# Layer normalisation around the mean of the first four feature blocks, its sums and squares added by TensorE between the last projections of the stage

## What is computed

```
def layer_norm(x, g, b):
    mu = jnp.mean(xf, -1, keepdims=True)
    var = jnp.mean(jnp.square(xf - mu), -1, keepdims=True)
    y = (xf - mu) * lax.rsqrt(var + LN_EPS)
    return y * g + b

x = layer_norm(ALPHA * x + m @ w_o, ln1_g, ln1_b)
h = jax.nn.silu(x @ w_gate) * (x @ w_up)
x = layer_norm(ALPHA * x + h @ w_down, ln2_g, ln2_b)
```

## Time and profile before

| | |
|---|---|
| median of 3 executions | 1194.69 us (1193.36 to 1196.69) |
| the profiled execution's own time | 1188.55 us |
| its span (first to last instruction) | 1186.7 us |
| PE busy in the span | 1039.2 us |
| mean granted TensorE clock | 0.936 of full speed |

### The profile page before, as it was taken

One profiled execution on the slowest core, in us unless ns is written; L12 is line 12 of the kernel. 1 busy time (PEld: TensorE's weight loads), 2 busy tenths in 40 slices (PEclk: granted clock), 3 DMA queues, 4 the chain that ended last, 5 costly groups with the idle time before them and its releaser, 6 DMA issues.

```text
span 1186.7 us, 22922 instructions
## 1 busy us (share of the span) xinstructions
PE 1039.2 (88%) x7438; PEld 965.6 (81%) x7438; DVE 555.3 (47%) x1070; ACT 495.1 (42%) x902; POOL 770.9 (65%) x1077
## 2 busy tenths in 40 slices
PE   5997798977798999999889968899669799999994
PEld 5996577765787999999779947787558699999993
DVE  2997946435624232210249987543446332222003
ACT  4333345533436544433353232654334364444334
POOL 6998216622493989998559971455127569999882
PEclk9988789988898999999989987999779989999997
DMA  8646458421152664444256534674002324444441
GB/s 305 219 164 216 128 179 281 169 92 54 43 191 82 212 238 163 177 160 169 81 183 219 172 96 133 207 266 174 36 36 102 129 108 160 172 167 160 175 145 76
DMA packets 78140, 185.07 MB, mean 156 GB/s; under 512 B 9283, under 2 KB 42435, under 8 KB 77507
## 3 DMA queue, kind: packets, MB, share of 16 engines
q1 hardware_dynamic: 74130, 171.22, 41.4%
q10 hardware_dynamic: 3744, 11.40, 2.7%
q0 software_dynamic: 144, 0.96, 0.2%
HBM read 170.97 MB, written 12.57 MB: 155 GB/s over the span
## 4 chain that ended last, share of the span: by engine, by line
POOL 63%; issue 35%; POOLq 1%; DMA 1%; ACT 0%; SPq 0%
POOL w_lo L567 57%; POOL hid L590 3%; POOL res L588 2%; POOLq L561 0%; DMA table<-page_table_in 0%; DMA wch<-weights_in 0%; POOLq L585 0%; POOLq L147 0%; POOL hid L588 0%; ACT w_hi L974 0%; POOL hid L591 0%; SPq L429 0%; POOLq L573 0%; SPq L170 0%; POOLq L578 0%
## 5 line engine op out<-in xcount | busy, mean ns | idle before, releaser
L567 POOL TENSOR_TENSOR w_lo<-wch,w_hi 128x256 fp32r<-128x256 f32 x940 | 705.8, 784 | 404.6 <-ACT w_hi L974 402.9
L627 PE MATMUL proj<-x_hi,w_hi 128*128 128x288 f32 x1376 | 416.7, 303 | 39.3 <-DVE x_lo L1598 17.3
L628 PE MATMUL proj<-x_hi,w_lo 128*128 128x288 f32 x1376 | 411.4, 299 | 0.0
L629 PE MATMUL proj<-x_lo,w_hi 128*128 128x288 f32 x1376 | 410.9, 299 | 0.0
L974 ACT ACTIVATE w_hi<-wch 128x1024 fp32r<-128x1024 f32 x235 | 248.3, 1057 | 230.3 <-PE proj L629 118.3
L627 PEld LDWEIGHTS proj<-x_hi,w_hi 128*128 128x128 f32 x1376 | 263.7, 192 | 51.1 <-issue 27.2
L628 PEld LDWEIGHTS proj<-x_hi,w_lo 128*128 128x128 f32 x1376 | 264.5, 192 | 0.0
L629 PEld LDWEIGHTS proj<-x_lo,w_hi 128*128 128x128 f32 x1376 | 263.9, 192 | 0.0
L1295 DVE SCALAR_TENSOR_TENSOR hid<-u_p,sm,hid 128x256 f32<-128x256 f32 x240 | 164.6, 755 | 3.4 <-DVE sq L1324 1.0
L645 PE MATMUL proj<-hid_lo,w_hi 128*128 128x288 f32 x352 | 104.2, 296 | 0.0
L643 PE MATMUL proj<-hid_hi,w_hi 128*128 128x288 f32 x352 | 103.8, 295 | 0.0
(11 more groups left out here) (236 smaller groups left out, 1298.3 us busy)
## 6 DMA issues: line engine op xcount, KB each, us to landing
wch<-weights_in SPq DMA_DIRECT2D x235, 512.0 KB, 3.2
pg<-cmp_pages_in SPq DMA_DIRECT2D x128, 128.0 KB, 2.6
pg<-slc_pages_in SPq DMA_DIRECT2D x128, 128.0 KB, 2.1
wn<-win_in SPq DMA_DIRECT2D x4, 2048.0 KB, 8.4
win_out<-wn ACTq DMA_DIRECT2D x4, 2048.0 KB, 8.1
hid<-w_in SPq DMA_DIRECT2D x2, 1024.0 KB, 5.9
kv_out<-kv ACTq DMA_DIRECT2D x2, 864.0 KB, 5.4
res<-xT_in SPq DMA_DIRECT2D x1, 1152.0 KB, 5.1
```

What stands on the lines that cost most here:

```text
L567: last = nc.gpsimd.tensor_tensor(lo[:, cols], raw[:, cols], hi[:, cols].bitcast(F32), ALU.subtract)
L627: mm(ps, hi[:, kb], x_hi[:, kb], start=kb == 0, stop=False)
L628: mm(ps, lo[:, kb], x_hi[:, kb], start=False, stop=False)
L629: last = mm(ps, hi[:, kb], x_lo[:, kb], start=False, stop=kb == KD - 1)
```

## The change

TensorE's sums move from behind the last projection to between the projections. To make that possible before the mean is known, the blocks are first shifted by an estimate of the mean, that of the first four blocks ("seed"): variance = mean of squares of the shifted values, minus the square of their mean. PE adds one seed matmul behind each of the projections 1 to 4, four square matmuls behind projection 5, and a mean and a square matmul for two blocks each behind projections 6 and 7 (`features_behind`): 4 + 4 + 8 = 16 for a normalisation. DVE subtracts the seed mean from the blocks as they come (`shifted`), forms the variance in one step (`var_ready`), and later subtracts the mean of the shifted values two blocks at a time, interleaved with the scaling and with `low`, which is `low_features`. ACT squares blocks 0 to 3 in two steps and 4 to 7 one by one, between the `high_part` calls. Three `warm` activations on one element per partition place the loads of the root's and of tanh's tables. In the down stage `high_part` of the next layer's chunks 0 and 1 come ahead of the last square. The convolution's normalisation does the same work under new names. The lines below leave blank lines and the signals' declarations out.

```diff
@@ -258,7 +259,9 @@
         ps_g = ps_t[:, 1, :]
         turn_ps = [ps_s[:, 0, :], ps_s[:, 1, :], ps_g] * 2
-        stat_ps = [a[:, 0:TOK] for a in (ps_g, ps_m, ps_s[:, 0], ps_s[:, 1], ps_s[:, 0], ps_s[:, 1])]
+        conv_mean, conv_var = ps_g[:, 0:TOK], ps_m[:, 0:TOK]
+        seed_ps, mean_ps, square_ps = ps_g[:, 0:TOK], ps_s[:, 0, 0:TOK], ps_s[:, 1, 0:TOK]
+        SEED = KD // 2
         def k(name):
             return cst[:, CONST[name]]
@@ -672,14 +678,46 @@
...
+            def seed_part(layer, which, kb):
+                o = (O_WO, O_DOWN)[which] + kb
+                pe.wait_ge(*out_read[o % 2](layer, o // 2 + 1))
+                last = mm(seed_ps, k("mean_c"), resv[:, kb], start=kb == 0, stop=kb == SEED - 1)
+                if kb == SEED - 1:
+                    stat_done.up(last)
+            def mean_part(layer, which, kb):
+                pe.wait_ge(*shifted(layer, 6 * which + kb - 1))
+                last = mm(mean_ps, k("mean_d"), resv[:, kb], start=kb == SEED, stop=kb == KD - 1)
+                if kb == KD - 1:
+                    stat_done.up(last)
+            def square_part(layer, which, kb):
+                pe.wait_ge(*squared(layer, 2 + 6 * which + (kb // 2 + 1 if kb < SEED else kb - 1)))
+                last = mm(square_ps, k("mean_d"), sqv[:, kb], start=kb == 0, stop=kb == KD - 1)
+                if kb == KD - 1:
+                    stat_done.up(last)
+            def features_behind(layer, which, n):
+                if 0 < n <= SEED:
+                    seed_part(layer, which, n - 1)
+                if n == SEED + 1:
+                    for kb in range(SEED):
+                        square_part(layer, which, kb)
+                if n > SEED + 1:
+                    for kb in (2 * n - 8, 2 * n - 7):
+                        mean_part(layer, which, kb)
+                        square_part(layer, which, kb)
@@ -932,22 +970,14 @@
-                for which in range(2):
-                    if which == 0:
-                        for n in range(KD):
-                            project_x(layer, O_WO + n, CH_IN + CH_MIX + n, 0 if n == 0 else None)
-                        first = O_WO
-                    else:
-                        for n in range(2 * KF):
-                            project_x(layer, O_GU + n, CH_IN + CH_MIX + CH_WO + n, KD if n == 0 else None)
-                        for n in range(KD):
-                            down(layer, n)
-                        first = O_DOWN
-                    def summed(kb):
-                        pe.wait_ge(*out_read[(first + kb) % 2](layer, (first + kb) // 2 + 1))
-                    statistics(layer, KD, resv, k("mean_d"), summed)
-                    statistics(layer, KD, sqv, k("mean_d"), lambda kb: pe.wait_ge(*squared(layer, 3 + 4 * which + kb // 2)))
+                for n in range(KD):
+                    project_x(layer, O_WO + n, CH_IN + CH_MIX + n, 0 if n == 0 else None)
+                    features_behind(layer, 0, n)
+                for n in range(2 * KF):
+                    project_x(layer, O_GU + n, FIRST_GU + n, KD if n == 0 else None)
+                for n in range(KD):
+                    down(layer, n)
+                    features_behind(layer, 1, n)
@@ -1031,17 +1061,30 @@
...
-                    act.wait_ge(*centered(layer, (4 * which - 2 if which else 0) + part + 1))
-                    do(sq[:, cols], source[:, cols], ACT.Square, squared, wait=False)
-            def norm_sd_root(layer, which):
...
+            def features_square(layer, which, n):
+                blocks = slice(2 * n, 2 * n + 2) if n < 2 else slice(n + 2, n + 3)
+                act.wait_ge(*shifted(layer, 6 * which + n + 1))
+                do(sqv[:, blocks], resv[:, blocks], ACT.Square, squared, wait=False)
+            def features_root(layer, which):
+                act.wait_ge(*stat_done(layer, 3 * which + 4))
+                do(sqv[:, 0], mean_ps, ACT.Square, mean_squared, wait=False)
+                act.wait_ge(*var_ready(layer, which + 1))
+                do(rstd, rstd, ACT.Sqrt, sd_ready)
@@ -1221,8 +1264,14 @@
                             do(x_hi[:, c], gate_a[:, c], ACT.Copy, x_hi_ready, wait=False)
                             if c % 2:
                                 high_part(layer, CH_IN + (KD + c) // 2 + PAIRS)
-                        for n in range(CH_IN + CH_MIX + PAIRS, CH_IN + CH_MIX + CH_WO + PAIRS):
-                            high_part(layer, n)
+                        for n in range(KD):
+                            high_part(layer, CH_IN + CH_MIX + PAIRS + n)
+                            if n == SEED:
+                                do(warm[:], eps[:, 0:1], ACT.Sqrt, wait=False)
+                                features_square(layer, 0, 0)
+                                features_square(layer, 0, 1)
+                            if n >= SEED:
+                                features_square(layer, 0, n - 2)
                     else:
                         for i in range(KF):
                             act.wait_ge(*out_done(layer, O_GU + 2 * i + 1))
@@ -1236,13 +1285,20 @@
                             if i == 2:
                                 act.wait_ge(*x_lo_ready(layer, 2 * KD))
                                 do(res[:], res[:], ACT.Copy, ax_ready, scale=ALPHA)
-                        for n in range(CHUNKS - CH_DOWN + PAIRS, CHUNKS):
-                            high_part(layer, n)
-                        high_part(layer + 1, 0)
-                    norm_sd_squares(layer, 1 + which, res[:], KD)
-                    if which == 1:
-                        high_part(layer + 1, 1)
-                    norm_sd_root(layer, 1 + which)
+                        do(warm[:], eps[:, 0:1], ACT.Sqrt, wait=False)
+                        n = SEED
+                        for c in range(CH_DOWN - 1):
+                            if n < KD - 1 and 8 * c + 7 >= KF * (n + 1) + 8:
+                                if n == SEED:
+                                    features_square(layer, 1, 0)
+                                    features_square(layer, 1, 1)
+                                features_square(layer, 1, n - 2)
+                                n += 1
+                            j = CHUNKS - CH_DOWN + PAIRS + c
+                            high_part(*((layer, j) if j < CHUNKS else (layer + 1, j - CHUNKS)))
+                        assert n == KD - 1
+                        features_square(layer, 1, n - 2)
+                    features_root(layer, which)
                     gn, bn = (s("g1"), s("b1")) if which == 0 else (s("g2"), s("b2"))
                     for c in range(KD):
                         if c % 2 == 0:
@@ -1253,6 +1309,7 @@
                             do(x_hi[:, c - 1], resv[:, c - 1], ACT.Copy, x_hi_ready, wait=False)
                     act.wait_ge(*x_ready(layer, KD * which + KD))
                     do(x_hi[:, KD - 1], resv[:, KD - 1], ACT.Copy, x_hi_ready, wait=True)
+                    do(warm[:], eps[:, 0:1], ACT.Tanh, wait=False)
                 high_part(layer + 1, 2)
                 act.sem_inc(act_order.sem, ACT_ORDER - act_order.count)
                 act_order.count = ACT_ORDER
@@ -1345,20 +1402,61 @@
...
-            def center(layer, which, source, n):
-                dve.wait_ge(*stat_done(layer, 2 * which + 1))
-                ps = stat_ps[2 * which]
-                for part in range(n // 2):
-                    two = source[:, 2 * part:2 * part + 2]
-                    do(v.tensor_tensor(two, two, ps.unsqueeze(1).broadcast_to([P, 2, TOK]), ALU.subtract), centered, wait=False)
-                dve.wait_ge(*centered(layer, centered.count))
-            def normalise(layer, which, source, n):
-                dve.wait_ge(*sd_ready(layer, which + 1))
...
+            def scale(two):
+                do(v.tensor_tensor(two, two, rstd.unsqueeze(1).broadcast_to([P, 2, TOK]), ALU.mult), normed, wait=False)
...
+            def features_norm(layer, which, low):
+                first = (O_WO, O_DOWN)[which]
+                dve.wait_ge(*ax_ready(layer, which + 1))
+                for n in range(KD):
+                    o = first + n
+                    dve.wait_ge(*out_done(layer, o + 1))
+                    read_out(o, v.scalar_tensor_tensor(out=resv[:, n], in0=bank[o % 2][:, 0:TOK], scalar=0.5, in1=resv[:, n],
+                                                       op0=ALU.mult, op1=ALU.add), wait=n >= SEED)
+                    if n == SEED:
+                        dve.wait_ge(*stat_done(layer, 3 * which + 3))
+                        for c in range(0, SEED, 2):
+                            two = resv[:, c:c + 2]
+                            do(v.tensor_tensor(two, two, seed_ps.unsqueeze(1).broadcast_to([P, 2, TOK]), ALU.subtract), shifted, wait=False)
+                    if n >= SEED:
+                        do(v.tensor_tensor(resv[:, n], resv[:, n], seed_ps, ALU.subtract), shifted, wait=n == KD - 1)
+                def subtract(c):
```

(38 more changed lines are left out.)

51 lines of the change are left out of this document (29 added, 22 removed).

## The result

| | before | after |
|---|---|---|
| median of the executions | 1191.88 us (1188.19 to 1196.69, 8) | 1202.78 us (1195.64 to 1208.44, 8) |
| the profiled execution's own time | 1188.55 us | 1201.59 us |
| its span | 1186.7 us | 1199.7 us |
| mean granted TensorE clock | 0.936 | 0.929 |

The ratio of the times is 1.0086, 95% interval [1.0058, 1.0114]: the change makes the kernel slower by 10.2 us (0.0086 x 1191.88). The forecast was +4.5 us.

A forecast was written before the change was run, and what follows sets the result against it. PE was taken to bound the projections, a chain of dependent steps the tails. Behind w_o +0.85 twice, boundary +0.65 and end +2.15 gave +4.5 us on the median 1194.69, so 1199.2 us; range 1193.0 to 1203.5.

The forecast's parts named there:

- 12 sums between projections, a stage: PE's full projection stream: 12 of 16 sum matmuls now stand between projections at 0.49 us each, 5.9 us added.
- six switches of format, a stage: PE going from fp32 sums back to fp32r projections: 0.05 us each, six times a stage, 0.3 us added.
- tail, T to scaling: From PE free behind the last projection (T) to first scaling: 5.65 us instead of 12.31, 6.65 us saved.
- restart behind w_o: First matmuls after the pause behind w_o: gaps and a later return of the clock cost 1.3 us a stage.
- boundary stage, T to the end of the last `x_lo`: Layer boundary: 6.65 us saved to scaling, 1.1 given back by the later last `x_lo`, the clock not counting.
- tail of the last stage, T to the span's end: Kernel end: 6.65 us saved, 1.1 given back, 1.5 added by a tanh table load ahead of the last `high_part`.
- The failed step: ACT's root table load (1.28 us) and squares of blocks 0 to 6, placed between `high_part` calls, cost nothing.
- the low bounds: Whole kernel, lower bounds everywhere (0.485 us a matmul, no switch cost, 0.5 for the restart): +1.3 us.
- the high ones: Whole kernel, upper bounds (0.25 us a switch, 2.5 for the restart): +11.7 us.
- That moved sums hide: Rival: slack in PE's stream hides the moved matmuls; free of charge, some 20 us gained, 1174. Chance 0.14.
- A clock low for longer: Rival: each of three restarts costs another 3 us or so at half speed; about +10 us, 1205. Chance 0.12.
- A tail that doesn't shorten: Rival: in the down stage a late load delays `high_part` and the last square; 3 us twice, +10, 1205. Chance 0.06.

The follow-up runs named there:

- e2: The changed kernel with the tile `warm` declared last, so all other tiles lie where they do in the kernel before; ratio 1.0050, +6.0 us.
- e11: The kernel before plus 12 unused fp32 matmuls of constants a stage where the change puts its sums, its own sums left in place; ratio 1.0172, +20.5 us.
- e1: The kernel before plus the unused one-element tile `warm` ahead of the constants, moving every later tile by 32 bytes; ratio 1.0034, +4.0 us.
- e12: The kernel before plus the unused tile declared right ahead of `w_hi`, so the weight tiles move and the constants and chunks stay; ratio 1.0046.
- e6: The kernel before plus ten matmuls of constants in the pause behind the squares' sums of each stage; ratio 1.0013.
- e8: The kernel before with feature normalisation squares rounded to fp32r and summed by fp32r matmuls, all sums still behind the last projection; ratio 0.9995.
- e5: e2 plus twelve fp32 matmuls of constants, results unused, in the pause behind the sums of each stage; ratio 1.0049.
- e3: e2 without the activation that loads the table of tanh early; ratio 1.0025.
- e7: e2 with the squares of the feature normalisations rounded to fp32r and summed by fp32r matmuls; ratio 0.9979.
- e9: e7 without the activation that loads the table of tanh early; ratio 0.9971.
- e4: e2 with VectorE's old order: all four subtractions ahead of the reciprocal, then four scalings, then eight `low`; ratio 1.0078.
- e10: e8 with the root's table load, and in the down stage `high_part` of the next layer's chunk 1, ahead of the squares; ratio 0.9957.

## Why the prediction came out as it did

It had the direction, and its range held the time; of the change's size it had about half. That the range held is partly luck. It was laid out around a median of 1194.69 us for the kernel before, and reached 8.8 us above it; the eight executions of the kernel before that go with the result have 1191.88, and the change added 10.2. Point by point:

| term, us | forecast | measured |
|---|---|---|
| 12 sums between projections, a stage | +5.9 | +5.84 to +5.85 with switching (e2, e11) |
| six switches of format, a stage | +0.3 | about 0, in the row above |
| tail, T to scaling | -6.65 | -6.4 (after) |
| restart behind w_o | +1.3 | +1.8 and +0.9 (e2), +2.3 (after, both layers) |
| boundary stage, T to the end of the last `x_lo` | -5.55 | -5.5 (e2) |
| tail of the last stage, T to the span's end | -4.05 | -4.3 (after) |
| place of the weight tiles | none | +4.0 (e1), +5.5 (e12) |

The boundary's row is a tail alone. What the whole boundary takes, from layer 0's last output to layer 1's first w_o output, is 5.5 us less in e2 than before (326.32 against 331.84), but over the kernels whose tail is as it was before (before, e1, e6, e8, e11, e12) this stretch is 329.7 to 336.3 us long, so that one pair doesn't price it.

**The path of the normalisation was right.** Without the moved tiles the stages give 4 x 5.84 - 4.5 - 5.5 (the 49th matmul behind w_o in e2, layers 0 and 1) - 5.5 (boundary) - 4.3 (end) = +3.6 us, and e2 was measured at +6.0 [3.2, 8.6]; the forecast was +4.5 for the same things. The statement that a matmul between projections "lengthens the stage by its own time", read from 25.00 busy of 25.00 us, is what e11 shows.

**The failed step is the one that costed the new activations only as work:** "The table load of the root, 1.28 us, and the squares of blocks 0 to 6 go onto ACT between `high_part` calls", and the sum, which has no term for anything outside the stages. As work no stage shows them costing anything: the stages are longer by the sums alone. But their operand is a new tile, declared ahead of the weights. That move makes a projection matmul 0.001 to 0.002 us longer. In e1 the w_o stages grow by 0.19 and 0.37 us, the down stages by 0.5 each, and every 48 matmuls of gate/up by 0.05 to 0.10, of which there are 44: 3.8 to 6.0 us in all, where e1 and e12 measured 4.0 and 5.5. It is as large as the whole forecast. Nothing in the trace of before could have priced it, but the declaration is part of the whole diff, and a bound for what it moves was not among the bounds.

**The smaller misses.** Scaling starts at T+5.92, not T+5.65, and the blocks come a little sooner behind it than laid out (the fourth is read 6.9 us behind the start of scaling, not 7.1). The restart behind w_o cost more than 1.3 in layer 0 and less in layer 1 of e2, inside the bounds of 0.5 to 2.5, because the return of the clock varies (T+15.7 to T+18.7 in e2 for much the same gaps). Switching back to fp32r was taken at 0.05 and is not to be seen. Two of its sums are a little off: the low bounds add up to +1.4, not +1.3, and the high ones, with 0.505 for a matmul too, to +12.3, not +11.7.

**The rivals.** That moved sums hide is excluded by e11. A clock low for longer was half right: 9.9 us at 0.50 instead of 5.7 behind w_o, but the 49th matmul paid 0.9 to 2.3 us for it (e2, after), not the 3 more of that rival, since PE must wait for blocks in that stretch anyway. A tail that doesn't shorten did not occur. The two profiled executions lie 13.0 us apart, 4.5 of it before the first w_o output (328.32 and 332.80); that output comes between 326.8 and 334.9 us over the kernels of this study without an order in it, so one pair of profiles can't be read as the change's size.

## What to carry to other kernels

Price an operation that moves out of a wait into a full stream at its full time, and compare with what the chain really gets back, the restart included: here 5.84 us went in for 4.1 to 5.5 that came back. Read a diff's declarations as well as its instructions: here a new scratch tile behind the large ones cost 4 us less than one ahead of them. Compare the step between two equal matmuls far from the change. When a step on the chain gets shorter, look at once for what stood hidden beside it (here a table load of 1.28 us) and move that too.

## What the runs showed that was not expected

A 32-byte move of the weight tiles, from a multiple of 64 bytes to half-way between, lengthens the fp32r matmul of 288 columns from 0.132 us to 0.133 or 0.134 (6.34 us for 48 became 6.41 and 6.45) and the kernel by 0.34% [0.20, 0.48] and 0.46% [0.27, 0.65]. The longer matmul comes in two sizes that change inside one execution (6.40 or 6.45 us for 48), and what chooses is open.

The granted clock can fall behind a filled pause when the restart itself has waits (e5). Behind an unfilled pause it was back 7.0 to 10.3 us after a restart with gaps (e2, e3, e7, e9, after), and 2.9 to 6.1 us after one with next to none (before, e1, e4, e8, e10, e11, e12); no profiled restart lies between.
